# Gate and up of a dense feed-forward with tokens as output rows in all six steps, and the product turned into the gate's PSUM banks

## The reference

```python
def swiglu(x, w_gu, w_down):
    g, u = jnp.split(x @ w_gu, 2, axis=-1)
    return (jax.nn.silu(g) * u) @ w_down
# x: (256, 1024) after RMSNorm; w_gu: (1024, 6144); w_down: (3072, 1024)
h = h + swiglu(rms_norm(h, norm_ffn_g[0]), ffn_w_gu[0], ffn_w_down[0])
```

## Time and profile before

| | us |
|---|---|
| median of 3 runs | 1143.67 |
| lowest, highest | 1142.41, 1144.84 |
| the profiled execution's own time | 1142.05 |
| its span, first to last instruction | 1140.3 |
| TensorE busy (matmuls) | 1107.2 |
| DVE busy | 872.9 |
| ACT busy | 720.4 |
| mean granted clock of TensorE, of full speed | 0.99 |

### The profile page before, as it was taken

The page is one execution under the profiler, slowest core; times in us unless marked ns, Lnnn a source line. Parts: engine busy times, 40 slices in busy tenths (PEclk is TensorE's granted clock), DMA queues, the critical chain, the costliest instruction groups (busy, mean ns, idle before and its releaser), DMA issues.

```text
span 1140.3 us, 19215 instructions
## 1 busy us (share of the span) xinstructions
PE 1107.2 (97%) x6834; PEld 969.6 (85%) x6834; DVE 872.9 (77%) x1053; ACT 720.4 (63%) x965; POOL 55.9 (5%) x31
## 2 busy tenths in 40 slices
PE   6999999999999999999999989999999999999995
PEld 5989989979999997989989977878788888888884
DVE  4976885864443557666785867999999999999995
ACT  4457764464444445456665456878888788887874
POOL 0200000000000000200000010101010101001010
PEclk9999999999999999999999998999999999999998
DMA  9955446556555655845445469999999999999951
GB/s 294 243 172 173 122 141 201 169 173 206 184 162 177 215 186 169 240 151 184 131 142 186 152 229 337 368 395 339 374 357 357 372 341 386 341 388 335 390 194 39
DMA packets 139338, 276.94 MB, mean 243 GB/s; under 512 B 26585, under 2 KB 26897, under 8 KB 139281
## 3 DMA queue, kind: packets, MB, share of 16 engines
q1 hardware_dynamic: 136832, 267.26, 69.7%
q0 software_dynamic: 2448, 8.91, 2.2%
HBM read 274.04 MB, written 2.10 MB: 242 GB/s over the span
## 4 chain that ended last, share of the span: by engine, by line
PE 83%; DVE 9%; ACT 4%; issue 3%; DMA 1%; DVEq 0%; SPq 0%; ACTq 0%
PE ps L1393 26%; PE ps L1395 25%; PE ps L1394 25%; DVE w_lo L855 3%; PE ps L1546 1%; DVE gates L864 1%; ACT w_hi L498 1%; PE ps L1778 1%; PE ps L1695 1%; PE ps L1574 1%; PE ps L1520 1%; PE ps L1684 1%; DMA h<-in_x_dram 1%; ACT p_t L650 1%; DVE yl L855 1%
## 5 line engine op out<-in xcount | busy, mean ns | idle before, releaser
L855 DVE TENSOR_TENSOR w_lo<-raw,w_hi 128x1024 fp32r<-128x1024 f32 x272 | 331.6, 1235 | 158.7 <-ACT w_hi L498 156.2
L498 ACT ACTIVATE w_hi<-raw 128x1024 fp32r<-128x1024 f32 x272 | 285.7, 1059 | 183.6 <-PE ps L1395 183.6
L1393 PE MATMUL ps<-xh,w_hi 128*128 128x256 f32 x960 | 274.5, 286 | 0.2 <-DVE w_lo L855 0.2
L1394 PE MATMUL ps<-xl,w_hi 128*128 128x256 f32 x960 | 271.6, 283 | 0.0
L1395 PE MATMUL ps<-xh,w_lo 128*128 128x256 f32 x960 | 271.6, 283 | 0.0
L1393 PEld LDWEIGHTS ps<-xh,w_hi 128*128 128x128 f32 x960 | 184.1, 192 | 3.3 <-issue 2.1
L1394 PEld LDWEIGHTS ps<-xl,w_hi 128*128 128x128 f32 x960 | 184.1, 192 | 0.4
L1395 PEld LDWEIGHTS ps<-xh,w_lo 128*128 128x128 f32 x960 | 184.0, 192 | 0.0
L1393 PE MATMUL ps<-w_hi,xh 128*128 128x512 f32 x448 | 177.8, 397 | 5.1 <-DVE w_lo L855 3.5
L1395 PE MATMUL ps<-w_hi,xl 128*128 128x512 f32 x448 | 174.7, 390 | 0.0
L1394 PE MATMUL ps<-w_lo,xh 128*128 128x512 f32 x448 | 174.5, 390 | 0.0
(11 more groups left out here) (225 smaller groups left out, 1561.5 us busy)
## 6 DMA issues: line engine op xcount, KB each, us to landing
mix<-in_moe_w_gu_dram SPq DMA_DIRECT2D x112, 512.0 KB, 7.6
raw<-in_w_in_dram SPq DMA_DIRECT2D x96, 512.0 KB, 4.2
raw<-in_moe_w_gu_dram SPq DMA_DIRECT2D x80, 512.0 KB, 5.8
mix<-in_moe_w_down_dram SPq DMA_DIRECT2D x80, 512.0 KB, 5.5
raw<-in_ffn_w_gu_dram SPq DMA_DIRECT2D x48, 512.0 KB, 4.1
raw<-in_w_branch_dram SPq DMA_DIRECT2D x24, 512.0 KB, 3.7
raw<-in_ffn_w_down_dram SPq DMA_DIRECT2D x24, 512.0 KB, 4.8
raw<-in_w_out_dram SPq DMA_DIRECT2D x16, 512.0 KB, 3.3
```

Of the source, the lines that this page charges most:

```text
L498: act.activation(halves(u)[0], src, ACT.Copy).then_inc(hi_done, 1)
L855: dve.tensor_tensor(w_l, place(u)[0], w_h.bitcast(F32), ALU.subtract).then_inc(lo_done, 1)
L1393: mm(dst, ah, bh, start=first, stop=False, skip_group_check=True)
L1394: mm(dst, ah, bl, start=False, stop=False, skip_group_check=True)
```

## The change

All six steps of gate and up are in the token form. The products of steps 2 to 6 are transposed by `turn_product` into banks 0 and 1, the gate's, once silu has read the next step's gate out of them: for steps 2 to 5 behind the seventh unit (k == 6) of the next gate-up, for step 6 behind the second unit of down 5. ACT's and DVE's split of an unturned product (`step_hi`, `step_lo`) is gone; `turned_hi` and `turned_lo` do it for every step, from the banks, at k == 9 and k == 10 of their loops. `down` waits for both halves of `al_ok` ahead of its first unit, and gate-up from step 3 on waits on `al_ok` before it fills the gate banks. TensorE's loop runs three times in place of four, and its last pass is written out.

```diff
--- before.py
+++ after.py
@@ -664,18 +664,11 @@
                     if RH <= k + AHEAD < U_MIX:
                         hi(B, k + AHEAD)
 
-            def step_hi(n, dst, i=0, per=0):
-
-                for b in range(2):
-                    act.wait_ge(prod_ok, 2 * i * per + (2 * n - 1 + b))
-                    act.activation(dst[:, 512 * b:512 * b + 512], prod_t[:, 512 * b:512 * b + 512],
-                                   ACT.Copy).then_inc(ah_ok, 1)
-
-            def turned_hi():
+            def turned_hi(n, bank, i=0, per=0, c0=0):
 
                 for t in range(TT):
-                    act.wait_ge(ft_ps, t + 1)
-                    act.activation(yh[:, 0:4, P * t:P * t + P], ps[:, 4 + t, :].rearrange("p (c s) -> p c s", c=4),
+                    act.wait_ge(ft_ps, TT * i * per + (TT * (n - 1) + t + 1))
+                    act.activation(yh[:, c0:c0 + 4, P * t:P * t + P], ps[:, bank + t, :].rearrange("p (c s) -> p c s", c=4),
                                    ACT.Copy).then_inc(ah_ok, 1)
 
             def dense():
@@ -695,23 +688,20 @@
                 for k in range(12):
                     hi(B + 8, k)
                     if k == 3:
-                        turned_hi()
+                        turned_hi(1, 4)
                     if k == 7:
                         silu(2, B + 12)
                 with act.Fori(0, FF_STEPS - 2) as i:
                     for k in range(12):
                         hi(B + 20, k, i, 12)
-                        if k == 2:
-
-                            act.wait_ge(unit_used, i * 12 + (B + 20))
-                            step_hi(2, yhf[:, 0:1024], i, 1)
                         if k == 7:
                             silu(3, B + 24, i)
+                        if k == 9:
+                            turned_hi(2, 0, i, 1)
                 for k in range(4):
                     hi(B + U_FF - 4, k)
                     if k == 0:
-
-                        step_hi(FF_STEPS, yhf[:, 1024:2048])
+                        turned_hi(FF_STEPS, 0, c0=BC)
 
             def experts(p):
                 B = BASE_MOE + p * E * U_EX
@@ -1148,25 +1138,18 @@
 
                 dve.wait_ge(unit_used, i * units + u_end)
                 if n > 1:
-                    dve.wait_ge(al_ok, 2 * i * per + 2 * (n - 1))
+                    dve.wait_ge(ft_ps, TT * i * per + TT * (n - 1))
                 for b in range(2):
                     dve.wait_ge(silu_ok, 2 * i * per + (2 * n - 1 + b))
                     dve.tensor_tensor(prod_t[:, 512 * b:512 * b + 512], ps[:, b_u + b, :],
                                       silu_t[:, 512 * b:512 * b + 512], ALU.mult).then_inc(prod_ok, 1)
 
-            def step_lo(n, i=0, per=0, at=0):
-                for b in range(2):
-                    dst = slice(at + 512 * b, at + 512 * b + 512)
-                    dve.wait_ge(ah_ok, 2 * i * per + (2 * n - 1 + b))
-                    dve.tensor_tensor(ylf[:, dst], prod_t[:, 512 * b:512 * b + 512], yhf[:, dst].bitcast(F32),
-                                      ALU.subtract).then_inc(al_ok, 1)
-
-            def turned_lo():
+            def turned_lo(n, bank, i=0, per=0, c0=0):
 
                 for t in range(TT):
-                    at = (slice(None), slice(0, 4), slice(P * t, P * t + P))
-                    dve.wait_ge(ah_ok, t + 1)
-                    dve.tensor_tensor(yl[at], ps[:, 4 + t, :].rearrange("p (c s) -> p c s", c=4), yh[at].bitcast(F32),
+                    at = (slice(None), slice(c0, c0 + 4), slice(P * t, P * t + P))
+                    dve.wait_ge(ah_ok, TT * i * per + (TT * (n - 1) + t + 1))
+                    dve.tensor_tensor(yl[at], ps[:, bank + t, :].rearrange("p (c s) -> p c s", c=4), yh[at].bitcast(F32),
                                       ALU.subtract).then_inc(al_ok, 1)
 
             def dense():
@@ -1179,19 +1162,19 @@
                     if k == 0:
                         product(1, 2, B + 8)
                     if k == 4:
-                        turned_lo()
+                        turned_lo(1, 4)
                 with dve.Fori(0, FF_STEPS - 2) as i:
                     for k in range(12):
                         lo(B + 20, k, i, 12)
                         if k == 0:
                             product(2, 2, B + 20, i, 1, 12)
-                        if k == 3:
-                            step_lo(2, i, 1)
+                        if k == 10:
+                            turned_lo(2, 0, i, 1)
                 for k in range(4):
                     lo(B + U_FF - 4, k)
                     if k == 0:
                         product(FF_STEPS, 2, B + U_FF - 8)
-                        step_lo(FF_STEPS, at=1024)
+                        turned_lo(FF_STEPS, 0, c0=BC)
 
             def build_g(p, e):
 
@@ -1621,13 +1604,13 @@
                 for k in range(4, 8):
                     unit_tokens(B, k, k - 4, 2)
 
-                def turn_product():
+                def turn_product(n, bank, i=0, per=0):
 
                     for t in range(TT):
-                        pe.wait_ge(prod_ok, t + 1)
+                        pe.wait_ge(prod_ok, TT * i * per + (TT * (n - 1) + t + 1))
                         for m in range(4):
-                            ins = pe.transpose(ps[:, 4 + t, P * m:P * m + P], prod_t[:, 512 * t + P * m:512 * t + P * m + P],
-                                               ident)
+                            ins = pe.transpose(ps[:, bank + t, P * m:P * m + P],
+                                               prod_t[:, 512 * t + P * m:512 * t + P * m + P], ident)
                         ins.then_inc(ft_ps, 1)
 
                 def gate_up(B, n, i=0, per=0):
@@ -1635,24 +1618,31 @@
                     for k in range(8):
                         if k == 0:
                             pe.wait_ge(silu_ok, 2 * i + 2 * (n - 1))
+                            if n > 2:
+                                pe.wait_ge(al_ok, 2 * i + 2 * (n - 2))
                         if k == 4:
                             pe.wait_ge(prod_ok, 2 * i + 2 * (n - 1))
-                        unit_columns(B, k, k % 4, 2 * (k // 4), (xhf, xlf), SEQ, i, per, last=KC - 1)
+                        unit_tokens(B, k, k % 4, 2 * (k // 4), i, per)
                         if n == 2 and k == 1:
-                            turn_product()
+                            turn_product(1, 4)
+                        if n > 2 and k == 6:
+                            pe.wait_ge(silu_ok, 2 * i + 2 * n)
+                            turn_product(n - 1, 0, i, 1 if n < FF_STEPS else 0)
 
                 def down(B, n, first, i=0, per=0):
+                    pe.wait_ge(al_ok, 2 * i + 2 * n)
                     for k in range(4):
-
-                        if k % 2 == 0:
-                            pe.wait_ge(al_ok, 2 * i + (2 if n == 1 else 2 * n - 1 + k // 2))
                         unit_wide(B, k, yh[:, k, :], yl[:, k, :], TT, first and k == 0, False, i, per)
+                        if n == FF_STEPS - 1 and k == 1:
+                            turn_product(FF_STEPS, 0)
 
                 gate_up(B + 8, 2)
                 down(B + 16, 1, True)
-                with pe.Fori(0, FF_STEPS - 2) as i:
+                with pe.Fori(0, FF_STEPS - 3) as i:
                     gate_up(B + 20, 3, i, 12)
                     down(B + 28, 2, False, i, 12)
+                gate_up(B + U_FF - 16, FF_STEPS)
+                down(B + U_FF - 8, FF_STEPS - 1, False)
                 last_wide(B, U_FF - 4, yh[:, BC:2 * BC, :], yl[:, BC:2 * BC, :], 2, (al_ok, 2 * FF_STEPS - 1))
 
             def rows_of_slots(e):
```

## The result

The changed kernel takes 1150.9 us (median of 5 runs, 1150.14 to 1151.68) against 1143.69 before: a ratio of 1.0062, 95% interval 1.0047 to 1.0077, so it is slower by 0.6%, little but clear of the noise. Its profiled execution is also at 1150.9 us, with a span of 1149.1.

A forecast was written before the change was run, and what follows sets the result against it. TensorE, busy 97% of the span, was taken as the bound. Terms -5.76 + 4.35 + 6.7 + 0.8 = +6.1 us, added to the 1143.67 us median, gave 1149.7 us; range 1146.4 to 1152.8.

The forecast's parts named there:

- units of gate and up: Steps 2 to 6: 36 of 40 units gain 0.16 us each in token form, four gain nothing; -5.76 us.
- five turns: Five added groups of 8 fp32 transposes in TensorE's own stream, uncovered, 0.87 us each; +4.35 us.
- waits ahead of four down projections: Down 2 to 5 wait for DVE's `turned_lo`, each starting 1.67 us late; +6.7 us.
- last turn's wait for the product: In down 5, the turn behind the second unit waits for DVE's product of step 6; +0.8 us.
- What I cost at nothing: Turned halves for unturned ones, new gate-up waits, tail hi and lo, weight loads, unrolled last pass: no added cost.
- Hidden conversions: Rival: the turned product's split ends by unit 7's end, so all four waits go; -0.65 us, 1143.0; chance 0.11.
- No gain: Rival: token units run as long as column units, 5.76 us more lost; 1155.4 us; chance 0.05.
- A falling clock: Rival: the clock falls ahead of every down projection for one unit; +9.6 us, 1159.3; chance 0.03.

The follow-up runs named there:

- form_alone: The kernel before with steps 2 to 6 of gate and up in token form and nothing turned, their transposes left out; 1137.29 us.
- turns_alone: The kernel before, forms unchanged, plus five turns (8 transposes each in gate-up 2 to 6) that nobody reads; 1147.93 us.
- last_turn_later: The changed kernel with split_earlier's edit and step 6's turn behind the third unit of down 5 (k == 2), not the second; 1141.25 us.
- split_earlier: The changed kernel with DVE's low part of the turned product at k == 9 in place of k == 10 in the loop; 1144.33 us.
- turn_earlier: The changed kernel with the turn one unit earlier on TensorE (k == 5), ACT and DVE as they are; 1147.60 us.

## Why the prediction was right, by its steps

The forecast was +6.1 us, the medians are 7.2 apart and the stage 6.74 longer; the mechanism is the one forecast. In the profiled executions, 8.8 us apart, 1.84 us lies ahead of the stage, 6.74 in it and 0.2 behind it. All sizes are of the stage. With 4.64 the shown terms are a chain of differences from the kernel before to the changed one, so that they add up to 6.74 by their making; what they show is the size of each.

| step | predicted | shown |
|---|---|---|
| units of gate and up | -5.76 | -5.60 (form_alone) |
| five turns | +4.35 | +4.27 between column units (turns_alone), +4.64 between token units (last_turn_later less form_alone) |
| waits ahead of four down projections | +6.7 | +6.98 (split_earlier) |
| last turn's wait for the product | +0.8 | +0.72 (last_turn_later) |
| sum | +6.1 | +6.37 with 4.27, +6.74 with 4.64 |

*The units.* Right, and for the reason given: the earlier trace rows hold in the new place, less than 0.2 us short in all.

*The turns.* Right in kind: nothing covers them. The size, 0.87 us, was read between column units, and there it holds (0.85). Between token units it is 0.93, and this is all that the sum of 6.37 lacks. last_turn_later and form_alone have the same units and the same waits of TensorE, and the one has five turns more; their stages are 4.64 us apart. Unit by unit, a turn and the unit behind it take 3.64 us there (319.92 to 323.56), 0.92 over a unit, and in turns_alone 3.74 (313.79 to 317.53), 0.86 over a unit. In both, the second matmul behind the turn comes 0.08 or 0.09 us late. The rest is the spacing: the 512-column matmuls behind a turn come 0.23 us apart, or 0.24 (320.70 to 323.01: ten in 2.31 us), before they are back at 0.2267, while the 256-column ones are at 0.12 at once.

*The waits.* Right in place, number and cause. Three of the four cost 1.76 us (down 2, 3 and 4, from the turn's start to the second down unit, against split_earlier), the fourth 1.68, for 1.67 forecast. In the three, TensorE started 0.13 us behind DVE's end (324.73 to 324.86) where I had 0.06, and in the fourth 0.055 (431.89 to 431.94). The three stand in TensorE's hardware loop and the fourth in the written-out pass. In the loop, the trace has an ALU_OP of TensorE's own between DVE's end and the matmul (324.77, at the wait for the unit's weights, whose count follows the loop counter), and in the fourth none. turn_earlier shows the same, 0.13 three times and 0.055 in the last. No run tested this by itself. The second matmul came 0.10 late where I had 0.08.

*The last turn.* Right; the trace of the changed kernel has the four transposes held from 437.53 to 438.04 and 0.22 us for one of them between the halves where 0.11 is usual.

*What I cost at nothing* held: no wait of TensorE for a weight other than in the second unit, none for silu, and no longer tail.

*The rivals.* Hidden conversions: not so, and split_earlier shows the one edit that makes it so, at 1144.3 us. No gain: not so. A falling clock: 1.00 in every stretch of the stage, in spite of four idle times of 1.39 to 1.46 us. Two sums of the prediction are slightly off: the terms of the hidden case add up to -0.61 us, not -0.65, and by its own working the range would end at 1153.1 and not at 1152.8; neither changes a reading. The Trainium skill's fixed cost of 2.5 ns a matmul ("TensorE: Matmul & The Clock Gate", Back-to-back issue gap, which gives it for an isolated matmul) would have made form_alone about 1 us faster than before; it is 5.6, so the trace's 13 ns decides.

## What to carry to other kernels

Where a product must be turned on the way to the next one, price three things apart: the transposes, which lie in TensorE's own stream; the instructions that make it ready; and what stands ahead of those in their engine's program. Here the first two left a gain and the third, one k in one `if` on DVE, cost more than the form could give. A longer distance between producer and consumer helps in full only where no instruction in between waits for the consumer's own stream: one unit more of it took 2.08 us here, the move on DVE 6.98.

## What the runs showed of the hardware that I had not expected

The profiled executions part ahead of the stage: this feed-forward part starts 1.84 us later in the changed kernel's (246.65 and 248.49), with the same code up to there. Most of it comes in the first 18 us: the starts of the first twelve matmuls of 512 columns run from 13.26 to 16.31 in the kernel before and from 13.44 to 17.88 in the changed one. The same matmuls of the kernel before and of the changed one:

```profile
13.61 0.40 PE L1394 MATMUL ps<-w_lo,xh 128*128 128x512 f32 x1
13.84 0.40 PE L1395 MATMUL ps<-w_hi,xl 128*128 128x512 f32 x1
14.08 0.39 PE L1393 MATMUL ps<-w_hi,xh 128*128 128x512 f32 x1
```

```profile
14.03 0.63 PE L1377 MATMUL ps<-w_lo,xh 128*128 128x512 f32 x1
14.46 0.63 PE L1378 MATMUL ps<-w_hi,xl 128*128 128x512 f32 x1
14.88 0.63 PE L1376 MATMUL ps<-w_hi,xh 128*128 128x512 f32 x1
...
17.02 0.56 PE L1378 MATMUL ps<-w_hi,xl 128*128 128x512 f32 x1
17.41 0.39 PE L1376 MATMUL ps<-w_hi,xh 128*128 128x512 f32 x1
17.65 0.40 PE L1377 MATMUL ps<-w_lo,xh 128*128 128x512 f32 x1
```

They are 0.23 us apart in one and 0.43 in the other, which is the distance that the earlier trace rows have at the lower clock. The views of stretches print a granted clock of 1.00 for both, but that isn't a measurement: the trace's record of the granted clock has its first entry, at full, at 11.80 us in the kernel before's execution and at 17.36 in the changed one's, and nothing ahead of it. 17.36 is where the distance goes from 0.43 to 0.23. Eight transposes ahead of either entry take 1.97 us (9.06 and 9.20) for 1.04 in the stage. So each execution starts at the lower of the two levels, and when it goes up differs, from 11.80 to 18.67 us in the nine. The stage starts earliest where the entry is earliest (246.65) and latest where it is latest (248.81), though not strictly in that order between them.

The same record has the fall of the earlier trace rows as 13.7 us at half clock in the kernel before, 17.1 in the changed one and 10.2 to 17.1 over the nine. These differences outside the stage are as large as some of the terms here, which is why one stage, cut out at its own ends, tells a tenth or two of a microsecond where single totals don't tell one.
